# Identity products on TensorE at four seams of a three-block float32 transformer kernel

## The reference, cut to what matters

```
    h = layer_norm(x, ln0_g, ln0_b)
    for l in range(DEPTH):
        mix = hybrid_mixer(h, ...)
        h = layer_norm(ALPHA * h + mix, ln1_g[l], ln1_b[l])
        ffn = grouped_moe(h, w_router, router_bias, w_gate[l], w_up[l], w_down[l])
        h = layer_norm(ALPHA * h + ffn, ln2_g[l], ln2_b[l])
```

## Time and profile before

| | |
|---|---|
| median of 3 runs | 3495.51 us (3495.16 to 3499.75) |
| the profiled execution | 3494.43 us, of which 3492.6 us are the span from first to last instruction |
| mean granted clock of TensorE | 0.915 |
| TensorE busy with products | 88% of the span |
| TensorE's share of the chain that ended last | 72% |

### The profile page before, as it was taken

How to read it: one execution, slowest core, us unless ns; L and a number is a source line. 1 busy time by engine, 2 the same in 40 slices (tenths; PEclk the granted TensorE clock), 3 DMA queues, 4 the chain that set the end, 5 groups by cost and what they waited for, 6 DMA issues and landing times.

```text
span 3492.6 us, 58593 instructions
## 1 busy us (share of the span) xinstructions
PE 3090.8 (88%) x24118; PEld 2488.9 (71%) x24118; DVE 1644.7 (47%) x2885; ACT 1220.7 (35%) x2083; POOL 831.1 (24%) x808
## 2 busy tenths in 40 slices
PE   6888898889898999999888788888889999888887
PEld 6767787778677878886677566666669998545565
DVE  3544544565524344342454364555565556432432
ACT  2323433433322243233433343433244343332341
POOL 4122121112112100001445355441000002513332
PEclk9888999989869999999899899999999999878998
DMA  3101111111004233331212122214325556301111
GB/s 122 29 28 35 29 41 30 31 32 41 29 25 164 84 121 94 93 97 52 61 55 64 43 64 65 60 58 142 91 78 174 164 164 181 119 20 46 43 46 60
DMA packets 94811, 259.79 MB, mean 74 GB/s; under 512 B 10672, under 2 KB 10672, under 8 KB 93264
## 3 DMA queue, kind: packets, MB, share of 16 engines
q1 hardware_dynamic: 81968, 209.11, 20.3%
q0 software_dynamic: 7680, 35.40, 3.0%
q10 hardware_dynamic: 4896, 11.54, 0.9%
HBM read 236.08 MB, written 19.92 MB: 73 GB/s over the span
## 4 chain that ended last, share of the span: by engine, by line
PE 72%; DVE 13%; ACT 10%; issue 3%; DMA 2%; POOL 1%; ACTq 0%; DVEq 0%; SPq 0%; POOLq 0%
PE psum L430 70%; DVE arena L362 6%; ACT arena L347 5%; ACT arena L355 3%; DVE arena L371 3%; PE psum L434 2%; ACT L343 1%; DMA ring<-in_w 1%; DVE arena L366 1%; ACT L347 1%; DVE arena L383 1%; POOL arena L362 1%; DVE arena L393 0%; DVE arena L386 0%; DMA arena<-in_x 0%
## 5 line engine op out<-in xcount | busy, mean ns | idle before, releaser
L430 PE MATMUL psum<-arena,ring 128*128 128x512 f32 (+3 forms) x6792 | 1640.3, 359 | 19.8 <-DVE arena L362 11.8
L430 PEld LDWEIGHTS psum<-arena,ring 128*128 128x128 f32 (+1 forms) x6792 | 1152.1, 194 | 215.7 <-issue 36.6
L430 PE MATMUL psum<-arena 32*32 32x32 f32 (+10 forms) x12500 | 934.2, 256 | 287.8 <-ACT arena L347 73.6
L430 PEld LDWEIGHTS psum<-arena 32*32 32x32 f32 (+7 forms) x12500 | 653.8, 143 | 525.0 <-issue 202.8
L430 PE MATMUL psum<-arena,arena 128*128 128x512 f32 (+3 forms) x3872 | 987.0, 351 | 32.6 <-DVE arena L362 11.2
L430 PEld LDWEIGHTS psum<-arena,arena 128*128 128x128 f32 (+2 forms) x3872 | 659.7, 188 | 155.6 <-issue 31.6
L355 ACT ACTIVATE arena<-psum 128x512 f32<-128x512 f32 (+14 forms) x660 | 301.5, 457 | 766.4 <-PE psum L430 617.5
L374 POOL CAST ring<-ring 128x512 fp32r<-128x512 f32 x332 | 221.3, 666 | 1208.9 <-DMA ring<-in_w 1199.9
L362 DVE TENSOR_TENSOR arena<-arena 128x528 f32<-128x528 f32 (+9 forms) x638 | 366.8, 575 | 229.8 <-ACT arena L347 123.1
L362 DVE TENSOR_TENSOR ring<-ring,arena 128x1024 fp32r<-128x1024 f32 (+1 forms) x250 | 293.6, 1174 | 338.1 <-ACT arena L355 335.1
L362 POOL TENSOR_TENSOR ring<-ring,ring 128x512 fp32r<-128x512 f32 x332 | 444.4, 1338 | 26.7
(11 more groups left out here) (51 smaller groups left out, 982.5 us busy)
## 6 DMA issues: line engine op xcount, KB each, us to landing
ring<-in_w SPq DMA_DIRECT2D x202, 512.0 KB, 3.5
ring<-in_w SPq DMA_DIRECT2D x356, 256.0 KB, 2.7
bg<-arena ACTq DMA_DIRECT2D x24, 256.0 KB, 2.1
yd<-arena ACTq DMA_DIRECT2D x10, 512.0 KB, 5.8
arena<-bg POOLq DMA_DIRECT2D x1, 3072.0 KB, 16.7
arena<-in_x SPq DMA_DIRECT2D x1, 2112.0 KB, 14.7
od<-arena POOLq DMA_DIRECT2D x8, 256.0 KB, 2.3
oy<-arena POOLq DMA_DIRECT2D x8, 256.0 KB, 2.3
```

Source lines behind the costliest of these rows:

```text
L430: self.last_ins = self.eng.matmul(out, l, r, start=start, stop=stop, skip_group_check=skip)
```

## The change

A method `busy` issues n products of the bfloat16 identity with itself, the moving side repeated four times to 512 columns, into a bank that nobody reads, and announces an event that only the bank's next user waits for. It is called four times: behind the announcement of `ln1`'s mean (20 products), behind `ln1`'s sum of squares (18), behind the bias tables (16) and behind `ln0`'s sum of squares (18). Nothing is taken away.

```
+    def busy(self, n, name, square):
+        b = self.bank(1, "busy", name)
+        for _ in range(n):
+            self.mm(self.ps[:, 512 * b:512 * b + 512], square[:], square[:].unsqueeze(1).to_broadcast([128, 4, 128]))
+        self.did("busy", name)
...
     K.P.did("mean", "ln1")
     K.P.drop(b)
+    K.P.busy(20, "mean", K.c["ident16"])
     pe_sum8(K, "ln1", m.O, T2)
+    K.P.busy(18, "ln1", K.c["ident16"])
     K.P.stage_end("pe", "branches")
...
     pe_tables(K)
+    P.busy(16, "results", c["ident16"])
     b = [P.bank(1, "normed", "ln2", k) for k in range(8)]
...
     pe_sum8(K, "ln0", m.O, T2)
+    K.P.busy(18, "ln0", K.c["ident16"])
     pe_mixers(K, m)
```

## The result

The changed kernel took 3511.55 us (median of 7 runs, 3503.7 to 3517.19), the kernel before 3495.71 (7 runs, 3493.41 to 3502.47). The ratio is 1.004, with a 95% interval of 1.0025 to 1.0055: slower by 0.4%. The forecast was 3497.8 us with a range to 3502.5, so it missed on the slow side.

A forecast was written before the change was run, and what follows sets the result against it. TensorE, 72% of the chain, was taken to bound the kernel by its queue and clock where it ends the chain. -2.1 + 4.4 + 0 + 0 = +2.3 us on the 3495.51 median gave 3497.8 us, within 3493 to 3502.5.

The forecast's parts named there:

- The 20 behind the mean: At ln1, the products wait for the mean's bank until centred 7 and delay the sum of squares: +4.4 us (4.3 to 4.7).
- I take it as kept in full: At ln0, the 48 products end 2.1 us earlier and downstream work, including POOL and SP weight work, keeps it: -2.1 us.
- `ln1`'s 18: Behind ln1's sum of squares, 3.96 us hidden in a 5.40 us pause; router paced by VectorE: 0 gain and cost.
- The 16 behind the tables: Behind the bias tables, the clock rises but falls again before n3: 0, at most -1.5 and -0.25 us.
- a spread of runs of some 2 to 3 us each way: Whole kernel: run-to-run scatter assumed around the forecast's own range of 3497.7 to 3499.6 us.
- The forecast's +2.3: Whole kernel: sum of the four calls' effects, -2.1 + 4.4 + 0 + 0 us, added to the median of 3495.51.
- The pause was not filled: Denies the rival that the 20 fill ln1's pause after the mean: -3.5 there, -5.6 in all, 3489.9 us; chance 0.11.
- The clock did rise on the bfloat16 products: Denies the slower rival's premise: clock stays down, the 20 cost 0.43 us each, nothing won at ln0: +8.6 us; chance 0.09.
- `ln0`'s gain is lost downstream: Rival: ln0's gain goes in weights or in a clock falling elsewhere: +4.4, 3499.9 us; chance 0.12.
- The transposes did not hold the clock to `n3`: Denies the rival that transposes behind the tables keep the clock up to n3: +0.6, 3496.1 us; chance 0.07.
- slower beyond doubt: Rival: the clock does not rise on the bfloat16 products at all: +8.6, 3504.1 us; chance 0.09.
- The 0.11 for slower: Whole kernel: chance given to a time above 3502.5 us, from the slower rival and a tail of the lost ln0 gain.

The follow-up runs named there:

- c4: Kernel before with no product added; ln1's sum of squares passes over the bank that waits for centred 7: 3494.67 us, ratio 0.9981 to before.
- e1: Kernel before plus only ln0's 18 products, with POOL's weight casts held until VectorE's last normed tile: 3500.57 us, ratio 0.9996 to before.
- e4: Kernel before plus only the 18 products behind ln1's sum of squares: 3504.48 us, ratio 1.0012 to before.
- f1: Changed kernel without the 20 products behind the mean, the other three calls kept: 3502.37 us, ratio 1.0004 to the kernel before.
- e3: Kernel before with c4 and e1 joined: mean's bank passed over, ln0's 18 products, POOL's casts later: 3492.85 us, ratio 0.998 to before.
- f2: f1 with the mean's bank also passed over: 3492.36 us, ratio 0.9977 to the kernel before.
- f4: c4 repeated, bank passed over and no product added to the kernel before: 3495.97 us, ratio 0.9988 to before.
- c3: Kernel before plus only the 20 products behind ln1's mean: 3506.42 us, ratio 1.0014 to before.
- d4: Changed kernel with the mean's bank passed over, so the 20 products take a free bank: 3501.03 us, ratio 1.001 to the kernel before.
- c2: Kernel before plus 72 products, all behind the last output product, none at a seam: 3512.01 us, ratio 1.0028 to before.
- c1: Kernel before, unchanged, profiled and timed a second time: 3502.59 us, ratio 1.0006 to before.

## Why the prediction was wrong

**The 20 behind the mean: right.** Forecast +4.4 us; the seam is +4.25, +4.15 and +4.17 in three traces of the change and +4.24 with these products alone. The bank's wait, its releaser, the place of the half-clock stretch and the sum's start 6.3 us behind the first product are as forecast. The price was taken as 0.22 and came out a little lower: 18 products take 4.05 us, so (4.05 - 0.40)/17 = 0.215, the lower bound. c4 adds what the prediction only argued: take the bank's wait away and 6.4 us are won.

**`ln0`: the step "I take it as kept in full" failed.** Forecast -2.1; measured -0.42, -0.43 and -1.10 in three traces of the change, -1.11 with the 18 alone, and about -0.5 when all traces with them are set against all without. The clock did stay up, and TensorE had caught up with VectorE. What I had not counted is that VectorE's own tiles depend on who works beside them: with TensorE earlier, the SP transfer and with it POOL's casts come earlier too, and POOL's work falls on VectorE's last tiles, 1.35 us each instead of 0.82. In the kernel before it had missed them by 0.40 us, which the trace showed. I had written that this work "moves with them" and had looked no further. e1 shows it as the cause: without the overlap 1.64 us for two, and the same slowdown at the next place of overlap.
The Trainium skill ("SBUF — State Buffer", Who interferes with whom) says that a VectorE instruction with two inputs in the on-chip memory contends with a GpSimd instruction that reads that memory, because the second input comes through a read interface that the two engines share. The row fits it in kind: `arena<-arena,arena` at 2.70 us for two beside a CAST and a TENSOR_TENSOR of POOL.

**`ln1`'s 18: right in the change**, where the pause is filled and the router is as far behind as before. It is not general: in e4 and f1, two of the seven traces with these products, the clock fell in the dense work behind the router, and the experts took 1.5 us more. **The 16 behind the tables: right at their own place**, with the clock up at their end and down again in the transposes. But `n3` is 1.96, 1.18 and 1.83 us longer in the traces of the change. That hangs on where the clock rises: 23.4 to 23.8 us after VectorE starts on the gathered results (`n3` +0.2 to +0.6), or 26.1 to 26.7 (+1.2 to +2.0). All five traces in which products wait for the mean's bank have the late rise, but so have five in which none do (e3, e4, f1, f2, f4). It may be the change's doing in part, and is not shown to be.

**The sum and its base: the step "a spread of runs of some 2 to 3 us each way" failed**, and it is the largest part of the miss. In 144 runs of the kernel before the mean is 3500.2 us and the standard deviation 6.6; the base of 3495.51 from three runs lay 4.7 below the mean. The seven runs beside the result had 3495.71 again, so they gave no warning. The forecast's +2.3 on 3500.2 would have been 3502.5, just at the range's end. With the seams as measured (`ln0`, `ln1`, experts and `n3` together +5.7, +4.9 and +4.9 us) it would have been 3505.1 to 3505.9. The changed kernel's 28 runs have a mean of 3509.3, so the change costs 9.1 us, with about 2.2 each way; taken set by set against the runs of before beside them it is 14.1, 8.9 and 10.1, in the mean over all runs 10.6. Of the 13.75 us between forecast and median, 4.7 are then the base, 2.2 the scatter of the seven changed runs (3511.55 against 3509.3), 2.6 to 3.4 the seams, and the rest is open.

**What stays open.** Some 3.9 us of these 9.1, more than the interval of 2.2, are in no seam, and 5.4 of the 10.6. c3, with the 20 alone, does not show it: its mean lies 4.9 us above the runs of before on its chip, and its `ln1` seam has 4.24 and `n3` 1.45. d4 does: its stages from `ln0` to `n3`, the mixers left out, are 4.2 us shorter, and its mean is 2.2 longer. The stages in which they could lie scatter too much from one trace to another to be read: block 1 from -0.7 to +11.4 us over all traces. The mixers behind `ln0` are 1.6 us longer in the mean of the seven traces with the products at `ln0` and 0.8 shorter in the nine without, which is a hint, but the uncertainty of that difference is as large as the difference. That added products cost something everywhere is not supported (c2, and f1 with 52 of the 72 at 1.0004). By what the mean's 20 would cost more than their own time inside the whole change is not shown.

**The rivals.** The pause was not filled: -5.6 did not come. d4, which does fill it, wins 3.87 at the seam and nothing that can be measured in the time. The clock did rise on the bfloat16 products. "`ln0`'s gain is lost downstream" is close to what happened, through VectorE instead of weights or clock, and in part. The transposes did not hold the clock to `n3`. The time was slower beyond doubt, but not by that rival's mechanism. The 0.11 for slower was too small because the spread it was built on was too small.

## What to carry to other kernels

A filler in an in-order queue is an instruction with needs of its own: ask which buffer it gets, when that was read, and who stands behind it; here it took over the wait that it was to use, and removing that wait won 6.4 us at the seam, while fillers alone gave no time that can be told to be below that of before. When a stage gets faster, look at what its end releases on the other engines, and whether those run into each other. Before a forecast of a few us rests on one trace or three runs, know how far runs of the same kernel lie apart, and compare traces stage by stage from a common instruction, with one stage that did not change among them.

## What the runs showed of the hardware

- The same instructions in block 1 take from 0.7 us less to 11.4 us more than in the trace of before (17 traces), and the granted clock over the first 1640 us is 0.92 in before and 0.90 in the change and in c1, which are both about 9 us longer there.
- The time of a run goes with its mean granted clock: correlation -0.90 over 137 runs of the kernel before.
- VectorE's 128x512 instructions with two inputs take 1.35 us instead of 0.82 beside POOL's CAST and TENSOR_TENSOR (the change), and a TENSOR_SCALAR 1.48 instead of 0.49 (e1).
- The clock can fall while TensorE is busy all the time. In each of the 18 traces it fell during the 16 instructions of the bias tables, which contract over 32 rows: in the change TensorE is busy with them for 6.00 of 6.00 us from 2991 to 2997, at 0.50. The 16 bfloat16 products behind them, which contract over 128 rows, began at 0.50 and saw 1.00 at their end. That the 32 rows are the reason is not shown; no run changed only that.
- Work that nobody waits for ends a kernel all the same: with 72 products behind the last tile the span ended 15.1 us behind VectorE's last instruction instead of 6.7 (c2).
